# A step's own work ahead of tile eviction and weight split in the second mixer's attention

## What is computed

```python
def _forgetting_attention(q, k, v, log_f):
    c = jnp.cumsum(log_f, axis=1).transpose(0, 2, 1)
    ...
    for i in range(T // Q_BLOCK):
        q0, q1 = i * Q_BLOCK, (i + 1) * Q_BLOCK
        s = jnp.einsum('bqhd,bkhd->bhqk', q[:, q0:q1], k[:, :q1]).astype(jnp.float32) * scale
        mask = (q0 + jnp.arange(Q_BLOCK))[:, None] >= jnp.arange(q1)[None, :]
        bias = jnp.where(mask, c[:, :, q0:q1, None] - c[:, :, None, :q1], 0.0)
        p = jax.nn.softmax(jnp.where(mask, s + bias, MASK_VALUE), axis=-1)
        outs.append(jnp.einsum('bhqk,bkhd->bqhd', p.astype(v.dtype), v[:, :q1]))
    return jnp.concatenate(outs, axis=1)
```

## Time and profile before

| | |
|---|---|
| median of 3 runs | 2081.66 us (2080.97 to 2082.47) |
| the profiled execution | 2078.73 us, its span 2077.0 us |
| mean granted TensorE clock in it | 0.965 of full |
| busy, share of the span | TensorE 92%, VectorE 52%, ScalarE 41%, GpSimd 8% |
| DMA | 84 GB/s mean over the span |
| tiles 17 to 27 with their attention steps | from about 1870 to 2001 us of the span |

### The profile page before, as it was taken

The page is one execution under the profiler, slowest core; times in us unless marked ns, Lnnn a source line. Parts: engine busy times, 40 slices in busy tenths (PEclk is TensorE's granted clock), DMA queues, the critical chain, the costliest instruction groups (busy, mean ns, idle before and its releaser), DMA issues. The chain is left out here.

```text
span 2077.0 us, 31442 instructions
## 1 busy us (share of the span) xinstructions
PE 1913.7 (92%) x12756; PEld 1709.9 (82%) x12756; DVE 1075.8 (52%) x1764; ACT 852.1 (41%) x1352; POOL 168.8 (8%) x186
## 2 busy tenths in 40 slices
PE   7999997689869999999989987899999998899988
PEld 6999997579759999999989965678888885787666
DVE  6667667685572343444453256544444347852243
ACT  6557741345571332333334244443333234324342
POOL 0001221122310000000000020000000002000101
PEclk9999999799989999999999999999999998999999
DMA  7223351214154223232322222222322322321101
GB/s 186 83 73 124 119 164 42 52 42 103 31 145 102 82 85 100 81 101 81 101 63 82 84 59 64 82 95 88 102 95 87 101 81 63 122 62 41 41 1 41
DMA packets 206366, 173.92 MB, mean 84 GB/s; under 512 B 42352, under 2 KB 181616, under 8 KB 206248
## 3 DMA queue, kind: packets, MB, share of 16 engines
q1 hardware_dynamic: 206248, 172.27, 27.9%
HBM read 161.40 MB, written 10.83 MB: 83 GB/s over the span
## 5 line engine op out<-in xcount | busy, mean ns | idle before, releaser
L162 DVE TENSOR_TENSOR main_wlo<-raw,main_whi 128x2048 fp32r<-128x2048 f32 x106 | 242.9, 2292 | 365.0 <-ACT main_whi L155 365.0
L155 ACT CAST main_whi<-raw 128x2048 fp32r<-128x2048 f32 x106 | 201.5, 1903 | 411.8 <-PE ps L177 410.5
L177 PE MATMUL ps<-ffn_xhi,main_whi 128*128 128x264 f32 (+1 forms) x768 | 205.2, 321 | 6.6 <-DVE ffn_xlo L647 6.6
L177 PE MATMUL ps<-ffn_xhi,main_wlo 128*128 128x264 f32 (+1 forms) x768 | 205.6, 322 | 0.0
L177 PE MATMUL ps<-ffn_xlo,main_whi 128*128 128x264 f32 (+1 forms) x768 | 205.4, 322 | 0.0
L177 PE MATMUL ps<-ffn_ahi,main_wlo 128*128 128x264 f32 (+1 forms) x768 | 205.2, 322 | 0.0
L177 PE MATMUL ps<-ffn_alo,main_whi 128*128 128x264 f32 (+1 forms) x768 | 205.0, 321 | 0.0
L177 PE MATMUL ps<-ffn_ahi,main_whi 128*128 128x264 f32 (+1 forms) x768 | 203.9, 320 | 0.0
L177 PE MATMUL ps<-gdn_xhi,gdnf_whi 128*128 128x264 f32 x768 | 162.4, 293 | 4.7 <-DVE gdn_xlo L518 4.4
L177 PE MATMUL ps<-gdn_xlo,gdnf_whi 128*128 128x264 f32 x768 | 158.9, 289 | 0.0
L177 PE MATMUL ps<-gdn_xhi,gdnf_wlo 128*128 128x264 f32 x768 | 158.6, 288 | 0.0
(11 more groups left out here) (498 smaller groups left out, 3777.8 us busy)
## 6 DMA issues: line engine op xcount, KB each, us to landing
raw<-in_ff_up_dram SPq DMA_DIRECT2D x32, 1024.0 KB, 5.4
raw<-in_ff_down_dram SPq DMA_DIRECT2D x32, 1024.0 KB, 5.0
raw<-in_gdn_in_dram SPq DMA_DIRECT2D x24, 1024.0 KB, 5.6
raw<-in_w_in_dram SPq DMA_DIRECT2D x14, 1024.0 KB, 5.2
raw<-in_mlstm_in_dram SPq DMA_DIRECT2D x12, 1024.0 KB, 5.3
raw<-in_gdn_out_dram SPq DMA_DIRECT2D x8, 1024.0 KB, 7.2
gdn_v_spilled<-gdnf_o SPq DMA_DIRECT2D x16, 264.0 KB, 2.2
gdn_z_spilled<-gdnf_o SPq DMA_DIRECT2D x16, 264.0 KB, 2.3
```

What stands on the lines that cost most here:

```text
L155: k.nc.scalar.copy(k.whi[:, slot % SPLIT_SLOTS, :], k.raw[:, slot, :]).then_inc(k.hi_done, 1)
L162: eng.tensor_tensor(k.wlo[:, s, :], k.raw[:, slot, :], k.whi[:, s, :].bitcast(F32), ALU.subtract).then_inc(k.lo_done, 1)
L177: mm = pe.matmul(ps[:, b, 0:k.width], w, x[:, half], start=first and n == 0, stop=last and n == 2)
```

## The change

In the tiles from 17 on, at x = 2, ScalarE does its part of the step first and evicts the tile after it. The split of the weights isn't made at x = 2 of the odd tile any more: ScalarE makes the high half after its part of the step at x = 0 of the next tile, and VectorE the low half after its part at x = 1 of the next tile. For the tiles before 17 the order stays. No instruction is added or removed.

```diff
--- before.py
+++ after.py
@@ -3315,12 +3315,21 @@
                     ins.then_inc(s.h_out, 1)
                 if j >= FOX0:
                     fox(fox_at(j, x))
+            def split(j):
+                if j % 2 == 1 and j // 2 + 2 <= SECN:
+                    split_hi(k, act, u0 + j // 2 + 2, ring(j // 2 + 2), t0 + j + 1)
             for j, x in hooks:
-                if x == 2:
-                    leave(j)
-                    if j % 2 == 1 and j // 2 + 2 <= SECN:
-                        split_hi(k, act, u0 + j // 2 + 2, ring(j // 2 + 2), t0 + j + 1)
-                beside(j, x)
+                if j < FOX0:
+                    if x == 2:
+                        leave(j)
+                        split(j)
+                    beside(j, x)
+                else:
+                    beside(j, x)
+                    if x == 0 and j > FOX0:
+                        split(j - 1)
+                    if x == 2:
+                        leave(j)
             for i in rest:
                 fox(i)
             split_hi(k, act, u0 + SECN + 1, ring(SECN + 1), t0 + nj)
@@ -3497,10 +3506,15 @@
                     normed(NCH - 1)
                 if j >= FOX0:
                     fox(fox_at(j, x))
+            def split(j):
+                if j % 2 == 1 and j // 2 + 2 <= SECN:
+                    split_lo(k, dve, u0 + j // 2 + 2, ring(j // 2 + 2))
             for j, x in hooks:
-                if x == 2 and j % 2 == 1 and j // 2 + 2 <= SECN:
-                    split_lo(k, dve, u0 + j // 2 + 2, ring(j // 2 + 2))
+                if x == 2 and j < FOX0:
+                    split(j)
                 beside(j, x)
+                if x == 1 and j > FOX0:
+                    split(j - 1)
             for i in rest:
                 fox(i)
             split_lo(k, dve, u0 + SECN + 1, ring(SECN + 1))
```

## The result

The changed kernel takes 2069.8 us (median), the kernel before 2081.66 us on the same chip. The ratio is 0.9941 with a 95% interval of 0.9925 to 0.9957, so 12.3 us less (9.0 to 15.6). The forecast was 2069.1. One of the five executions of the changed kernel took 2134.07 us at a mean granted clock of 0.918, where the others had 0.966 to 0.968; it is left out of the ratio, and the median of the other four is 2069.2.

The account below looks back on a forecast made before the run. In tiles 17 to 27 TensorE was taken as the bound, held up five times by ScalarE's exponential behind eviction, cast, subtraction and maximum. Waits -7.45, clock -4.8, end of tile 27 -0.3: 2081.66 - 12.55 = 2069.1 us, range 2065.0 to 2074.5.

Parts of the forecast that it names:

- The waits of TensorE: Transposes in tiles 18, 20, 22, 24 and 26 wait for ScalarE's exponential; all five waits go, -7.45 us.
- The slack of about 2 us: Time between the third step's exponential and TensorE's need for it: 2.3 us in tile 18, 2 to 2.6 assumed for odd tiles.
- The clock: TensorE's clock falls after three of the five waits; regaining 1.6 us for each gives -4.8 us, bounds 0 and -8.0.
- The draw of the falls: Which of the five waits brings a clock fall varies from run to run; three in this trace, 0 to -8.0 us.
- the rival that it falls there anyway: The clock falls in tiles 17 to 27 or the final stage without the waits: 2073.9 us, chance 0.15.
- The end of tile 27: The last copy, for which TensorE waits, goes ahead of the 0.59 us eviction: -0.3 us.
- Cast and subtraction in their new places: ScalarE's cast (1.91 us) and VectorE's subtraction (2.29 us) are covered by idle gaps and slack in the next tile: cost 0.
- The distance of 2.9 us between median and profiled execution: Before the change, the median of the timed runs lay 2.9 us above the profiled execution; assumed unchanged afterwards.

Follow-up runs that it names:

- experiment 7: Changed kernel with VectorE's subtraction done three times in each of the five places: 2088.0 us, ratio 1.0027 against the kernel before.
- experiment 2: Changed kernel with only VectorE's order new; ScalarE evicts and casts ahead of its step as in the kernel before: 2068.5 us.
- experiment 3: Changed kernel with the split still moved on, but ScalarE's eviction ahead of its step again: 2069.4 us.
- experiment 1: Changed kernel with the step first, but the split kept at x = 2 of the odd tile instead of moved to the next tile: 2069.0 us.
- experiment 6: Changed kernel with VectorE's subtraction done twice in each of the five places: 2068.9 us.
- experiment 4: Changed kernel with the new order only for tiles 22 to 27, the old one for the tiles before: 2076.3 us.
- experiment 5: Changed kernel with the new order only for tiles 17 to 21, the old one from tile 22 on: 2073.1 us.
- experiment 8: Changed kernel without GpSimd's mask additions, and so without the causal mask inside the diagonal chunks: 2069.4 us in a single execution.
- experiment 9: Changed kernel with the mixer's last split moved into the final stage: 2065.3 us, against 2069.3 us for the changed kernel beside it.

## Why the prediction was right, step by step

- **The waits of TensorE, -7.45 us.** Right. All five are gone, none took their place, and experiment 7 shows that they would have come back had the chain been 4.6 us longer instead.
- **The slack of about 2 us**, read off the even tile 18. Right, and the most useful number of the working: experiments 2 and 3 stay within it, experiments 1 and 6 pass it by at most 0.64 us in a place and cost 1.6 us of the stretch at most, experiment 7 leaves it by up to 2.9 us.
- **The clock, -4.8 us.** The mechanism was right, the size of a fall somewhat small. 13.27 - 7.45 - 0.37 (the end of tile 27) leaves 5.45 us for three falls, 1.8 each, not 1.6. The other kernels agree. Experiment 4: 125.78 - 117.27 = 8.51, less 4.85 of waits, 3.66 for two falls. Experiment 5: 4.94, less 2.59 of waits and 0.37, 1.98 for one. Experiment 7: 19.55, less 11.4, 8.2 for four falls, the only wait without one being that of 1.32 us; by the rows of the clock the long fall after the wait of 2.70 us took 3.1 of it. These sizes are what is left of the stretch; the clock's rows alone give about 1.7 a fall, and the rest no row names. I had scaled the windows down after a check on one third of a tile, and the window after the third wait ended at 1940.5, before the clock was back at about 1941.
- **The draw of the falls.** Right: the same wait was followed by a fall in one kernel and not in another. Of 15 waits between 0.95 and 2.9 us in the four traces that have them, 10 were followed by a fall: all six of 1.97 us and more, both of 1.47, one of the two of 1.64, one of the three of 1.23 to 1.32, and none of the two of 0.95. The waits of 0.64 us and less in experiments 1 and 6 were followed by none, and in the eight traces without a longer wait the clock is at 2.4 GHz over the whole stretch, so the rival that it falls there anyway is out. Hence the number of falls in the timed executions of the kernel before is not fixed, and with it a part of the gain: 12.3 us by the ratio, less 7.8, leaves two to three falls at the middle of the interval, and its ends, 9.0 and 15.6, leave one to four. That the forecast lies within a microsecond of the result is therefore in part luck: the range of 0 to 5 falls was known beforehand, their number in the timed executions was not.
- **The end of tile 27, -0.3 us.** Right: 0.37 and 0.36 in experiments 2 and 3, where it is undone.
- **Cast and subtraction in their new places, 0.** Right: the stretch is as short without the lengthened subtractions (experiment 8), and TensorE's list has no wait for an exponential. The reading behind the cast was too generous: 2.57 us isn't the shortest gap ahead of an exponential. The trace of before has 2.33 us at 1925.89 and 2.23 at 1999.83, and its own row at 1897.21 has 1.04. In the changed kernel 0.52 to 1.59 us of idle time were left behind the cast.
- **What I gave too much weight.** The prediction treated the parts as if all belonged to the gain. Experiments 1 and 2 show that VectorE's order carries nearly all of it, that ScalarE's eviction and cast may stay where they were at a cost of 0.37 us, and that the move to the next tile adds 1.2 us.
- **The distance of 2.9 us between median and profiled execution.** I left it as it was; the median of after is 1.2 above its profiled execution. The traces suggest that such a distance is mostly the drift of the stages ahead of the stretch, which begins at times 5.7 us apart. Where it begins earliest, at 1872.92 (before) and 1873.05 (experiment 3), the profiled execution lies 2.9 and 3.1 us below the median; where it begins latest, at 1878.61 (experiment 4), it lies 3.5 us above. What makes those stages drift stays open.

## What to carry to other kernels

When one engine waits now and then for a short step of another, look at what stands ahead of that step on the queue, and compare the places where the wait occurs with like places where it doesn't: the second kind gives the slack after the change before anything is built. Price a wait of about a microsecond or more on TensorE with its chance of a fall of the clock; here the falls cost 5.5 us on top of 7.45 us of waits. And measure a local change by the length of its own stretch in the trace, since the start of the stretch wandered by nearly half of the whole gain.

## What the runs showed of the hardware

- A subtraction with two SBUF inputs on VectorE (128 by 2048) took 2.58 us with a GpSimd addition of 0.46 us (128 by 128) beside it and 2.28 without, in one kernel, and 2.28 in all places when the addition was left out. The Trainium skill ("SBUF — State Buffer", Who interferes with whom) says that the two contend, and calls it an exclusive lock. The trace agrees that they contend. But 0.43 us of the addition lay beside the subtraction and cost it 0.30 us, and the additions took 0.45 to 0.46 us before and after; a lock that stops one of the two until the other ends would have cost 0.43 us or more.
- TensorE's clock fell after waits as short as 1.23 and 1.47 us, but not after every wait of that size. A fall cost 1.8 to 2.0 us of the stretch in the kernel before and experiments 4 and 5; in experiment 7 one lasted about twice as long. After the idle time at the block's end the matmuls with `w_out` ran at 1.2 GHz for 3.3 us in the changed kernel and 5.4 us in experiment 9.
